# Local attention: both key heads in one unit, and small products gathered into fewer slots

## What is computed

```
h = rmsnorm(x);  z = h @ w_in                      # one projection, split by columns
ya = gMLP(gelu(za))                                # A: spatial product in blocks of 128 tokens
yb = local attention(bq, bk, bv, sinks)            # B: 8 query heads, 2 key heads, chunks of 64,
                                                   #    a chunk sees itself and the one before it
yc = indexed attention(cq, latent, iq, ik, iw)     # C: 4 heads, one key head, top 64 keys by index score
yd = pooling mixer(zd)                             # D: causal means over 2, 4, 8, 16 tokens
x = x + (sum over b of sigmoid(gate_b) * (y_b @ w_out_b)) @ w_o
x = x + (silu(g) * u) @ w_down,  g, u = rmsnorm(x) @ w_gate_up
```

## Time and profile before

| | |
|---|---|
| median of three runs | 814.96 us (814.76 to 815.02) |
| the profiled execution | 815.25 us, of which its span is 813.5 us |
| TensorE busy | 805.1 us, 99% of the span |
| VectorE, ScalarE, GpSimd busy | 559.7, 406.1 and 56.6 us |
| DMA | 144.38 MB, mean 177 GB/s |
| granted TensorE clock | full throughout (1.0) |

### The profile page before, as it was taken

The page is one execution under the profiler, slowest core; times in us unless marked ns, Lnnn a source line. Parts: engine busy times, 40 slices in busy tenths (PEclk is TensorE's granted clock), DMA queues, the critical chain, the costliest instruction groups (busy, mean ns, idle before and its releaser), DMA issues.

```text
span 813.5 us, 10282 instructions
## 1 busy us (share of the span) xinstructions
PE 805.1 (99%) x3872; PEld 658.0 (81%) x3872; DVE 559.7 (69%) x854; ACT 406.1 (50%) x568; POOL 56.6 (7%) x103
## 2 busy tenths in 40 slices
PE   8999999999999999999999999999999999999998
PEld 6788777778888888888888887787788888888886
DVE  7799789877576554566568887898675754565443
ACT  5966655454274434444366644755543643444431
POOL 5850000000000000000005100000000000000000
PEclk9999999999999999999999999999999999999999
DMA  8654536545466555666663625474446555666541
GB/s 301 215 162 136 183 120 208 206 140 183 130 221 206 178 185 161 207 202 192 164 230 116 232 79 182 133 254 156 155 156 207 179 183 166 210 193 198 165 155 52
DMA packets 98976, 144.38 MB, mean 177 GB/s; under 512 B 11112, under 2 KB 62064, under 8 KB 98928
## 3 DMA queue, kind: packets, MB, share of 16 engines
q1 hardware_dynamic: 98928, 143.73, 54.6%
HBM read 142.54 MB, written 1.05 MB: 177 GB/s over the span
## 4 chain that ended last, share of the span: by engine, by line
PE 94%; DMA 2%; DVE 1%; ACT 1%; issue 1%; SPq 1%; ACTq 0%; DVEq 0%
PE big L1537 19%; PE big L1541 19%; PE big L1540 19%; PE mix L1541 10%; PE mix L1537 10%; PE mix L1540 10%; DMA w_raw<-in_w_in 1%; PE mix L1913 1%; PE mix L1581 1%; PE mix L1672 1%; DMA w_raw<-in_w_gate_up 1%; PE mix L1605 1%; PE mix L1593 1%; PE mix L1625 1%; PE mix L1658 1%
## 5 line engine op out<-in xcount | busy, mean ns | idle before, releaser
L738 ACT ACTIVATE w_hi<-w_raw 128x2048 fp32r<-128x2048 f32 (+2 forms) x140 | 255.0, 1827 | 155.4 <-DMA w_raw<-in_w_gate_up 89.6
L1049 DVE TENSOR_TENSOR w_lo<-w_raw,w_hi 128x2048 fp32r<-128x2048 f32 (+3 forms) x142 | 304.6, 2160 | 29.2 <-ACT w_hi L738 27.9
L1537 PE MATMUL big<-w_hi,act_hi 128*128 128x512 f32 (+2 forms) x476 | 185.7, 390 | 2.1 <-DVE w_lo L1049 2.1
L1541 PE MATMUL big<-w_hi,act_lo 128*128 128x512 f32 (+2 forms) x476 | 181.6, 381 | 0.0
L1540 PE MATMUL big<-w_lo,act_hi 128*128 128x512 f32 (+2 forms) x476 | 181.5, 381 | 0.0
L1537 PE MATMUL mix<-w_hi,act_hi 128*128 128x512 f32 x352 | 137.4, 390 | 0.0
L1541 PE MATMUL mix<-w_hi,act_lo 128*128 128x512 f32 x352 | 137.1, 390 | 0.0
L1540 PE MATMUL mix<-w_lo,act_hi 128*128 128x512 f32 x352 | 137.0, 389 | 0.0
L1537 PEld LDWEIGHTS big<-w_hi,act_hi 128*128 128x128 f32 x476 | 89.5, 188 | 22.6 <-DVE w_lo L1049 3.7
L1323 DVE TENSOR_TENSOR y_h_lo<-mix,y_h_hi 128x256 fp32r<-128x256 f32 x44 | 16.6, 420 | 127.7 <-ACT y_h_hi L968 127.7
L1541 PEld LDWEIGHTS big<-w_hi,act_lo 128*128 128x128 f32 x476 | 89.4, 188 | 17.2
(11 more groups left out here) (210 smaller groups left out, 718.6 us busy)
## 6 DMA issues: line engine op xcount, KB each, us to landing
w_raw<-in_w_in SPq DMA_DIRECT2D x44, 1024.0 KB, 5.1
w_raw<-in_w_gate_up SPq DMA_DIRECT2D x88, 512.0 KB, 4.8
w_raw<-in_w_down SPq DMA_DIRECT2D x22, 1024.0 KB, 4.9
w_raw<-in_w_o SPq DMA_DIRECT2D x8, 1024.0 KB, 4.9
w_raw<-in_b_w_out SPq DMA_DIRECT2D x4, 1024.0 KB, 6.3
w_raw<-in_w_in SPq DMA_DIRECT2D x4, 512.0 KB, 4.1
w_raw<-in_a_w_out SPq DMA_DIRECT2D x4, 512.0 KB, 3.5
w_raw<-in_d_w_out SPq DMA_DIRECT2D x4, 512.0 KB, 3.4
```

What stands on the lines that cost most here:

```text
L738: nc.scalar.activation(high(u)[:, a:b], arrived(u)[:, a:b], ACT.Copy).then_inc(hi_ready, 1)
L1049: nc.vector.tensor_tensor(low(u)[:, a:b], arrived(u)[:, a:b], high(u)[:, a:b].bitcast(F32), ALU.subtract).then_inc(lo_ready, 1)
L1537: ins = nc.tensor.matmul(dst[:, 0:w], xh, wh, start=first and n == 0, stop=False)
L1541: ins = nc.tensor.matmul(dst[:, 0:w], xl, wh, start=False, stop=end)
```

## The change

The local branch has two units in place of four: one for each block of 128 queries, with both key heads. A unit's scores fill both of its banks (eight heads' worth: per bank four parts of 128 columns, ordered key head, then chunk), its weights fill `probs` seen as eight rows of 128 (`weights_b`), its turned weights take two banks, its values one bank of 512 columns. The number of small products stays as it was. `row` grows from 4 to 8 columns, the two sinks DMAs become four (one for each pair of a and o), and VectorE has ten counted steps fewer for a layer.

Slots move as the tables show. S, T and Y of B are now in 14, 17, 19 and 19, 22, 23; S and T of C stay, and Y of C's first unit goes from 26 to 27. The small products kv, wT and TK now share slot 8, idx0 and TQ slot 11, idx1 and yaT slot 13, S of the first unit goes with ydT into 14, TC and TJ go with T into 17. On TensorE the turns of TQ come ahead of idx0 in slot 11. VectorE's softmax steps of a slot now come ahead of its y_d_lo (the ydT step), and the mean of ck's sums goes from slot 8 to 9.

```diff
-ATTN = [("B", 0, 0), ("B", 0, 1), ("B", 1, 0), ("B", 1, 1), ("C", 0, 0), ("C", 0, 1)]
+ATTN = [("B", 0), ("B", 1), ("C", 0), ("C", 1)]
 def turned_blocks(i):
-    return 1 if ATTN[i][0] == "B" else ATTN[i][2] + 1
+    return 2 if ATTN[i][0] == "B" else ATTN[i][1] + 1
...
-PE_AT = {"latT": 5, "TI": 5, "kv": 7, "wT": 9, "TK": 8, "idx0": 10, "TQ": 11, "idx1": 14, "TC": 15, "TJ": 16,
+PE_AT = {"latT": 5, "TI": 5, "kv": 8, "wT": 8, "TK": 8, "idx0": 11, "TQ": 11, "idx1": 13, "TC": 17, "TJ": 17,
          "spatial": 12, "mixed": 12, "yaT": 13, "ydT": 14}
-S_AT = [13, 15, 17, 19, 23, 25]
-T_AT = [15, 17, 19, 21, 25, 27]
-Y_AT = [17, 19, 21, 23, 26, 28]
+S_AT = [14, 19, 23, 25]
+T_AT = [17, 22, 25, 27]
+Y_AT = [19, 23, 27, 28]
...
-             (("yaT",), 3), (("S", 0, 0), 0), (("S", 0, 1), 1), (("idx", 1, 0), 0), (("idx", 1, 1), 1),
-             (("ydT", 0), 2), (("ydT", 1), 3), (("TC",), 3)]
+             (("yaT",), 3), (("idx", 1, 0), 0), (("idx", 1, 1), 1), (("S", 0, 0), 0), (("S", 0, 1), 1),
+             (("ydT", 0), 2), (("ydT", 1), 3), (("TC",), 0), (("TJ", 0), 1)]
...
+        weights_b = probs[:].rearrange("p h (a k) -> p (h a) k", a=2)
...
-                    *((sinks[HD * a:HD * a + HD], b_sinks[l].rearrange("(k a o) -> a k o", k=2, a=2)[a].partition_broadcast(HD))
-                      for a in range(2)),
+                    *((sinks[HD * a:HD * a + HD, o],
+                       b_sinks[l].rearrange("(k a o) -> a o k", k=2, a=2)[a, o].partition_broadcast(HD))
+                      for a in range(2) for o in range(2)),
... (exps)
-                        for cc in range(2):
-                            h, n = 2 * odd + cc, chunk_keys(tb, cc)
-                            e = nc.scalar.activation(probs[:, h, 0:n], mix[:, bank, cc * P:cc * P + n], ACT.Exp,
+                        for part in range(4):
+                            h, n = 4 * odd + part, chunk_keys(tb, part % 2)
+                            e = nc.scalar.activation(weights_b[:, h, 0:n], mix[:, bank, part * P:part * P + n], ACT.Exp,
... (softmax_in; softmax_out likewise over eight heads)
-                    s_in = mix[:, first:first + 2, 0:2 * P].rearrange("p o (c k) -> p o c k", c=2)
+                    s_in = mix[:, first:first + 2, :].rearrange("p o (x k) -> p (o x) k", k=P)
... (VectorE's steps)
-                if s == 8:
+                if s == 9:
                     mean_of_sums(l, "ck", HD)
... (now ahead of the ydT step, before behind it)
+                for i in range(len(ATTN)):
+                    if s == T_AT[i] - 1:
+                        softmax_out(l, i)
+                for i in range(len(ATTN)):
+                    if s == S_AT[i]:
+                        softmax_in(l, i)
... (TensorE, values)
-                            for cc in range(2):
-                                n, cols = chunk_keys(tb, cc), slice(kv * HD, (kv + 1) * HD)
...
+                            for kv in range(2):
+                                for cc in range(2):
+                                    n, cols = chunk_keys(tb, cc), slice(kv * HD, (kv + 1) * HD)
+                                    v = v_mid[:, cols] if (tb, cc) == (1, 0) else v_b[0:n, tb, cols]
+                                    for odd in range(2):
... (TensorE, scores: the same loop over kv around cc and odd)
... (TensorE, turned weights)
-                                n = chunk_keys(tb, h % 2) if m == "B" else P
...
+                                    n = chunk_keys(tb, h % 2)
+                                    src = weights_b[:, 4 * (h // 2) + 2 * k + h % 2, 0:n]
```

More of the change, by code:

```diff
@@ L204 @@
            22: (1, 5, 7), 23: (1, 7, 8)}
-DVE_STEPS = 132
+DVE_STEPS = 122
 class Signal:
@@ L260, in trunk_kernel @@
         top8 = sb("top8", [P, 8])
-        row = sb("row", [P, 8, 4])
+        row = sb("row", [P, 8, 8])
         za = probs_t[:].rearrange("p t h q -> p t (h q)")
@@ L1224, in softmax_in @@
             def softmax_in(l, i):
-                m, kv, tb = ATTN[i]
+                m, tb = ATTN[i]
+                heads = 8 if m == "B" else 4
                 for odd in range(2):
@@ L1230, in softmax_in @@
                     first = mix_bank("S", i, 0)
-                    s_in = mix[:, first:first + 2, 0:2 * P].rearrange("p o (c k) -> p o c k", c=2)
-                    r0, r1, r2 = (row[:, k, :].rearrange("p (o c) -> p o c", o=2) for k in range(3))
-                    sink = sinks[:, kv, :].unsqueeze(2).to_broadcast([P, 2, 2])
-                    step(l, nc.vector.tensor_reduce(r0, s_in, AX_X, ALU.max))
+                    s_in = mix[:, first:first + 2, :].rearrange("p o (x k) -> p (o x) k", k=P)
+                    r0, r1, r2 = (row[:, k, :].rearrange("p (x c) -> p x c", c=2) for k in range(3))
+                    sink = sinks[:].rearrange("p o k -> p (o k)").unsqueeze(2).to_broadcast([P, 4, 2])
+                    step(l, nc.vector.tensor_reduce(row[:, 0, :], s_in, AX_X, ALU.max))
                     step(l, nc.vector.scalar_tensor_tensor(out=r0, in0=r0, scalar=SCALE, in1=sink,
@@ L1261, in softmax_out @@
                     dve.wait_ge(*exp_ready.nth(l, tb + 1))
-                step(l, nc.vector.reciprocal(row[:, 6, :], total))
-                if m == "B" and tb == 0:
-                    parts = [(probs[:, cc::2, 0:chunk_keys(tb, cc)], row[:, 6, cc::2]) for cc in range(2)]
-                else:
-                    n = 2 * CHUNK if m == "B" else keys(tb)
-                    parts = [(probs[:, :, 0:n], row[:, 6, :])]
+                step(l, nc.vector.reciprocal(factor, total))
+                if m == "C":
+                    parts = [(probs[:, :, 0:keys(tb)], factor)]
+                elif tb == 0:
+                    parts = [(weights_b[:, cc::2, 0:chunk_keys(tb, cc)], factor[:, cc::2]) for cc in range(2)]
+                else:
+                    parts = [(weights_b, factor)]
                 for p, r in parts:
@@ L1407, in steps @@
                         ins.then_inc(mix_drained[bank].sem, 1)
[L1408 to L1413, removed]
                 if s == PE_AT["yaT"]:
                     y_low(l, 1, y_ac_hi[:], y_ac_lo[:], 0.5, "yaT")
-                for i, (m, kv, tb) in enumerate(ATTN):
+                for i, (m, tb) in enumerate(ATTN):
                     if s == Y_AT[i]:
-                        k0 = 2 * kv if m == "B" else 0
+                        k = 4 if m == "B" else 2
                         hi, lo = Y[m]
-                        y_low(l, 3 + i, hi[:, k0:k0 + 2, tok(tb)], lo[:, k0:k0 + 2, tok(tb)], 1.0, "Y", i, cols=2 * P)
+                        y_low(l, 3 + i, hi[:, 0:k, tok(tb)], lo[:, 0:k, tok(tb)], 1.0, "Y", i, k=k, cols=k * P)
                 if s == WO - 1:
@@ L1619, in attention @@
                             pe.wait_ge(*mix_is_free(l, "Y", i)).then_inc(alone_pe, 1)
-                            for cc in range(2):
-                                n, cols = chunk_keys(tb, cc), slice(kv * HD, (kv + 1) * HD)
[L1622 to L1628, removed]
+                            for kv in range(2):
[3 more added lines that the diff above has]
+                                    for odd in range(2):
+                                        dst = mix[HD * odd:HD * odd + HD, bank, 2 * kv * P:2 * (kv + 1) * P
+                                                  ].rearrange("p (a t) -> p a t", a=2)
+                                        ins = nc.tensor.matmul(
+                                            dst[:, :, cc * CHUNK:(cc + 1) * CHUNK], v,
+                                            probs_t[0:n, kv, 2 * odd + cc, :].rearrange("p (a t) -> p a t", a=2),
+                                            start=True, stop=True)
                             ins.then_inc(mix_full[bank].sem, 1)
@@ L1645, in attention @@
                             pe.wait_ge(*mix_is_free(l, "S", i, odd))
[L1646 to L1655, removed]
-                                else:
-                                    window = window.rearrange("p (d k) -> p d k", d=2)
-                                ins = nc.tensor.matmul(dst, chunked_queries(kv)[half, c * P:(c + 1) * P], window,
-                                                       start=True, stop=True)
-                                if cc == 1:
-                                    ins.then_inc(mix_full[bank].sem, 1)
+                        for kv in range(2):
+                            for cc in range(2):
+                                c = 2 * tb + cc
+                                for odd in range(2):
+                                    half = slice(HD * odd, HD * odd + HD)
+                                    bank, part = mix_bank("S", i, odd), 2 * kv + cc
+                                    dst = mix[:, bank, part * P:(part + 1) * P].rearrange("p (d k) -> p d k", d=2)
+                                    window = qk_t[half, 7 + kv, max(c - 1, 0) * CHUNK:(c + 1) * CHUNK]
+                                    if c == 0:
```

(7 more changed lines are left out.)

53 lines of the change are left out of this document (27 added, 26 removed).

## The result

The changed kernel takes **816.91 us** (median of 9 runs, 816.68 to 819.70); the kernel before took 814.58 in the 9 runs beside it. The ratio is 1.0033, 95% interval 1.0025 to 1.0041: 2.3 us slower. The forecast was 814.4, with a range that ended at 816.4, and it gave "slower" (above 816.6) 0.09: the time lies outside the range, in a case that was held unlikely.

The account below looks back on a forecast made before the run. TensorE, busy 99% of the span, was taken to bound the kernel. Terms -2.04 - 0.90 + 1.40 + 0.96 = -0.58 us on the profiled 815.25 gave 814.7, with the median 0.29 lower 814.4 us; range 812.0 to 816.4.

Parts of the forecast that it names:

- Everything else on VectorE and ScalarE (...) is off the chain: VectorE and ScalarE: ten short steps fewer, wider ones instead, wT's drain a slot earlier; counted as costing nothing.
- Small products, -2.04: TensorE, both layers: merged S and Y runs of B and fewer ends of half-array runs save 1.02 us a layer.
- Slot 11's way from turns into a half-array run: TensorE, slot 11: turns ahead of a half-array run cost 0.10 us, bounds 0 and 0.15.
- Waits of slot 15, -0.90: Slot 15: TensorE's two waits, for VectorE's first merge and unit 17's low part, go; saves 0.45 us a layer.
- Slot 13, +1.40: Slot 13, both layers: idx1 waits 0.7 us for bank 1, as idx0's later drains delay ScalarE's squares and VectorE's `gated`.
- Slot 4, +0.96: Slot 4, layer 0: two more sinks DMAs delay unit 5's load by 1.39 us and TensorE's start by 0.96.
- Slot 22, nothing: Slot 22: T of B's second unit just does not wait for VectorE's softmax_out; spare 0.2 us, no cost.
- the prediction's first rival: The new waits of slots 13 and 4 stay out: only -2.94 us is left, 812.0; chance 0.14.
- The rival on the slower side, VectorE late in slot 21: Late softmax_out of unit 1 holds TensorE at slot 22 in both layers; 817.2 at 1.6 us late; chance 0.09.

Follow-up runs that it names:

- the kernel with three parts undone: Changed kernel with `row` allocated last (128-byte place left), squares of v ahead of idx's drains in slot 11, and two sinks DMAs: 812.21 us, 0.9964 of the kernel before.

## Why the prediction was wrong

**The step that failed** is the sentence "Everything else on VectorE and ScalarE (...) is off the chain". It costed the rest of the diff at nothing and looked at instructions alone. The growth of `row` from four to eight columns stands in the diff and was given no term; it moves the y tiles by 128 bytes and makes 768 products on them start 3 to 5 ns further apart each. That costs 2.8 us when done alone in the kernel before and gives 3.0 when undone in the changed one. With it the forecast of 814.4 becomes 817.2 to 817.4, against 816.91. The two profiled executions add up the same way: -0.58 as forecast, +0.1 for the errors of its other terms, +3.1 for the y tiles and -0.5 for the stray wait of before at 227 us make 2.1, the difference of the spans.

The other steps, each with its measurement:

- *Small products, -2.04.* Scores 1.09 (1.06), values 1.47 and 1.02 (1.46 and 1.01): as written, together 0.08 a layer above the forecast. Slot 11's way from turns into a half-array run was taken at 0.10, between 0 and 0.15. The chain of the kernel with three parts undone shows it whole: the eight turns at 0.87, idx0 at 0.65 and the big product behind it at 0.43, each the length that it has elsewhere. So it costs 0:

```profile
69.22 0.87 PE mix L1600 x8
70.09 0.65 PE mix L1612 x8
70.74 0.43 PE big L1544
```

  The Trainium skill (TensorEngine Tiling (Array Packing), Key Properties) says that changing the tiling mode drains the engine, and names no direction; rows here show a price on the way out of the half array (0.15 to turns, 0.20 to big products) and none on the way in from turns. So the cost of 0.15 that the prediction worked out by that page is not borne out.
- *Waits of slot 15, -0.90.* Gone, as written.
- *Slot 13, +1.40.* 1.4 in the waits, 1.3 when its cause is taken away. The cause is the one named: idx's drains ahead of the squares on ScalarE.
- *Slot 4, +0.96.* 1.11 in the pair of traces, 0.8 in the mean of all; 1.0 when done alone, 1.2 when undone, by the times. The load went out 1.29 later where 1.39 was forecast, and that is in part luck: the sinks' issues grew by 2.18, not 1.39, but began 0.39 earlier, and the issues behind them took 0.50 less.
- *Slot 22, nothing.* VectorE's last step of softmax_out ends at 143.43 (its timeline, first row below), TensorE's T starts at 143.63 by its own (second row; 143.79 in the chain) out of a steady row of products, with no wait. The spare was 0.2 by the forecast and is 0.2 to 0.4.

```profile
142.20 1.23 DVE L1275 TENSOR_TENSOR probs<-probs,row 128x1024 f32<-128x1024 f32 x1
```

```profile
143.63 1.03 PE L1685 MATMUL mix<-ident,probs 128*128 128x128 f32 x8
```

- *Sum.* The kernel that undoes the three costs is 2.93 us faster than before; the prediction's first rival, with the two waits out, had -2.94. The kernel with only `row` put back measures 814.08, where 814.4 was forecast. The interval of the first reaches from 2.0 to 4.0 us, so agreement to 0.01 is luck; and the small errors of the terms (+0.08 a layer for the merged runs, -0.10 for slot 11, -0.2 to +0.2 for slot 4) nearly cancel. The mechanisms are what the traces bear out.

The rival on the slower side, VectorE late in slot 21, did not come about: the kernel is slower for a reason that no case of the prediction had.

## What to carry to other kernels

Go through the allocations of a diff as well as its instructions: a tile that grows moves all that is allocated after it, and on a kernel whose TensorE is busy 99% of the time a few nanoseconds on each of 768 products outweighed a careful saving elsewhere. Put small tiles that may grow at the end, or keep the stationary and the streamed operands of a product at one fixed distance, and when a timing is off everywhere by 1 or 2%, compare the distance between starts of the same product by operand, not only the waits. When a transfer is moved back in a queue, look up who waits for the count that it belongs to: here the parameters' count, and what was to be a gain became a loss of 1.7 us.

## What the hardware showed

The distance between starts of a 128x512 product in fp32r depends on where its stationary tile lies relative to the tiles allocated ahead of it, the streamed weight rings among them, and repeats after 256 bytes in steps of 64: 227 ns at best and on act tiles, 233 ns at worst, 2.6%. The records of weight loads don't show it (188 ns in both kernels for the y_h tiles), the distance of the products does. The Trainium skill (SBUF — State Buffer, Who interferes with whom) gives TensorE two independent read ports, one for the moving operand and one for weight loads, and says that PE never waits on anyone; read as it stands, that leaves no reason for the place to matter. The measurement decides: it does, by 2.8 us in 815. Why is not settled. Two reads of the same engine that meet would fit the dependence on the relative place alone, but no run tells them from something else that both share, such as ScalarE's and VectorE's writes into the rings, and which of the weight rings or act tiles is the other side was not tried apart.
